# Other PSUM banks and another order for the Fourier transforms inside the Hyena layer's input projection

## What is computed

```python
def hyena_mixer(h, w_in, short_w, short_b, f_w1, f_b1, f_w2, f_b2, f_w3, f_freq, f_skip, w_out):
    seq = h.shape[1]
    v, x1, x2 = jnp.split(depthwise_conv3(h @ w_in, short_w, short_b), 3, axis=-1)
    h_freq = hyena_filters(seq, f_w1, f_b1, f_w2, f_b2, f_w3, f_freq)

    def long_conv(u, n):
        uf = u.astype(jnp.float32)
        y = jnp.fft.irfft(jnp.fft.rfft(uf, n=2 * seq, axis=1) * h_freq[:, n], n=2 * seq, axis=1)[:, :seq]
        return (y + uf * f_skip[n].astype(jnp.float32)).astype(u.dtype)

    z = x1 * long_conv(v, 0)
    z = x2 * long_conv(z, 1)
    return z @ w_out
```

## Time and profile before

| | us |
|---|---|
| median of 3 runs | 2073.58 |
| the 3 runs | 2073.58, 2074.35, 2070.02 |
| the profiled execution, its own time | 2070.28 |
| its span, first to last instruction | 2068.5 |

### The profile page before, as it was taken

One profiled execution on the slowest core, in us unless ns is written; L12 is line 12 of the kernel. 1 busy time (PEld: TensorE's weight loads), 2 busy tenths in 40 slices (PEclk: granted clock), 3 DMA queues, 4 the chain that ended last, 5 costly groups with the idle time before them and its releaser, 6 DMA issues.

```text
span 2068.5 us, 32463 instructions
## 1 busy us (share of the span) xinstructions
PE 1998.6 (97%) x12754; PEld 1619.4 (78%) x12754; DVE 1267.2 (61%) x1567; ACT 904.4 (44%) x1250; POOL 168.6 (8%) x190
## 2 busy tenths in 40 slices
PE   7989999999999999999999999999999999999999
PEld 6688678878678878978878678877767888897887
DVE  7764655557665545665667655577885554475553
ACT  4453244434544434444545544434434444444442
POOL 2242100010010001000002011002100000000000
PEclk9989999999999999999999999999999999999999
DMA  8321265545256665465455247653324555455554
GB/s 296 116 63 44 64 216 185 182 163 194 82 178 200 183 201 173 164 201 185 164 184 193 82 160 222 204 178 128 103 82 138 187 183 184 162 165 191 183 170 145
DMA packets 92752, 335.95 MB, mean 162 GB/s; under 512 B 11198, under 2 KB 11332, under 8 KB 92335
## 3 DMA queue, kind: packets, MB, share of 16 engines
q1 hardware_dynamic: 85536, 311.62, 45.3%
q0 software_dynamic: 7120, 22.95, 3.9%
HBM read 332.43 MB, written 1.05 MB: 161 GB/s over the span
## 4 chain that ended last, share of the span: by engine, by line
PE 86%; DVE 8%; POOL 2%; issue 2%; ACT 2%; DMA 0%; SPq 0%; DVEq 0%; ACTq 0%; POOLq 0%
PE acc L360 41%; PE acc L437 21%; PE acc L413 9%; PE acc L896 2%; DVE w_lo L1521 2%; PE aux L817 1%; PE aux L610 1%; PE aux L852 1%; POOL rstd L2325 1%; POOL stat L2328 1%; PE aux L884 1%; PE aux L457 1%; DVE token_scratch L1597 1%; PE aux L873 1%; DVE stat L1579 0%
## 5 line engine op out<-in xcount | busy, mean ns | idle before, releaser
L1521 DVE TENSOR_TENSOR w_lo<-w_raw,w_hi 128x1024 fp32r<-128x1024 f32 x588 | 716.3, 1224 | 583.7 <-ACT w_hi L1143 579.1
L1143 ACT ACTIVATE w_hi<-w_raw 128x1024 fp32r<-128x1024 f32 x588 | 620.2, 1059 | 798.6 <-PE acc L360 471.3
L360 PE MATMUL acc<-w_hi,operand_hi 128*128 128x512 f32 x1344 | 535.5, 398 | 26.6 <-DVE operand_lo L1676 12.2
L360 PE MATMUL acc<-w_hi,operand_lo 128*128 128x512 f32 x1344 | 526.1, 391 | 0.0
L360 PE MATMUL acc<-w_lo,operand_hi 128*128 128x512 f32 x1344 | 525.2, 391 | 0.0
L360 PEld LDWEIGHTS acc<-w_hi,operand_hi 128*128 128x128 f32 x1344 | 253.7, 189 | 88.4 <-DVE operand_lo L1542 15.0
L360 PEld LDWEIGHTS acc<-w_hi,operand_lo 128*128 128x128 f32 x1344 | 253.4, 189 | 54.4
L360 PEld LDWEIGHTS acc<-w_lo,operand_hi 128*128 128x128 f32 x1344 | 254.1, 189 | 50.6 <-issue 0.5
L437 PE MATMUL acc<-w_hi,hidden_hi 128*128 128x512 f32 x528 | 210.2, 398 | 0.0
L437 PE MATMUL acc<-w_hi,hidden_lo 128*128 128x512 f32 x528 | 208.5, 395 | 0.0
L437 PE MATMUL acc<-w_lo,hidden_hi 128*128 128x512 f32 x528 | 208.5, 395 | 0.0
(11 more groups left out here) (471 smaller groups left out, 2098.2 us busy)
## 6 DMA issues: line engine op xcount, KB each, us to landing
w_raw<-in_weights SPq DMA_DIRECT2D x588, 512.0 KB, 3.3
ln_gain<-in_gains POOLq DMA_DIRECT2D x7, 512.0 KB, 5.1
bias_at<-in_rpb POOLq DMA_DIRECT2D x12, 256.0 KB, 5.4
ln_gain<-in_ln_g POOLq DMA_DIRECT2D x4, 512.0 KB, 3.9
ln_bias<-in_ln_b POOLq DMA_DIRECT2D x4, 512.0 KB, 5.3
vec_rw<-in_vec POOLq DMA_DIRECT2D x3, 512.0 KB, 6.6
l_rw<-in_lora SPq DMA_DIRECT2D x1, 1152.0 KB, 10.6
iclr_rw<-in_xT SPq DMA_DIRECT2D x2, 512.0 KB, 4.6
```

The costliest lines, as they stand in the source:

```text
L360: mm = pe.matmul(acc[:, 2 * pair + t, :], (ah, al)[x][:, kt, t * P:(t + 1) * P], W[w][:, s, kk * 512:(kk + 1) * 512], start=(kt == 0 and ( ...
L1143: act.activation(whi[:, s, :], raw[:, s, :], ACT.Copy).then_inc(w_hi[s], 1)
L1521: dve.tensor_tensor(wlo[:, s, :], raw[:, s, :], whi[:, s, :].bitcast(F32), ALU.subtract).then_inc(w_lo[s], 1)
```

## The change

Nothing is computed that was not computed before, and no instruction is dropped. Three things differ.

1. **Banks.** Before, `turn_cv(j)` wrote HI for j = 0 to 3, LO for 4 and FAR for 5. Now it writes the banks of its own block, NEAR for an even j and FAR for an odd one. The transforms, spectra and `norm` keep to the four banks of LO and HI, but for `idft(1, 0)`, which stays in NEAR.
2. **Waits.** Since block j + 2 accumulates in the banks in which `turn_cv(j)` wrote, TensorE now waits ahead of blocks 2 and 3 for `folded`, and ahead of blocks 4 and 5 for `cv_copied` (`banks_taken`). The waits of `turn_cv(1)`, `(2)`, `(3)` and `(4)` for banks of the transforms are gone; others are moved as the banks ask for it.
3. **Order.** `norm(1)` moves from (4, 2) to (4, 1); `idft(0, 1)` with `gated(0, 1)` from (5, 0) into block 4, (4, 2); `dft(1, 0)` and `dft(1, 1)` with their products one quarter ahead, to (5, 0) and (5, 1); `spectrum(1, 1, 1)` and its butterfly from (4, 3) to (5, 2); `dft(1, 2)` behind the end of block 5.

The diff; in ScalarE's and VectorE's tables only the lines that name the places are left:

```diff
     def dft_banks(n, r):
-        return ((HI, LO, HI, LO), (HI, HI, LO, HI))[n][r]
+        return ((HI, HI, LO, HI), (HI, LO, HI, LO))[n][r]
     def idft_banks(n, c):
-        return ((LO, LO), (NEAR, LO))[n][c]
+        return ((LO, LO), (NEAR, HI))[n][c]
     def cv_banks(j):
-        return (HI, HI, HI, HI, LO, FAR)[j]
+        return (NEAR, FAR)[j % 2]
+    def spectrum_order(f, part, c):
+        return 4 + 2 * c + (1 - part) if f else 2 * (1 - part) + c
     def spectrum_banks(f, part, c):
-        return (LO, LO, LO, LO, HI, LO, HI, NEAR)[spectrum_order(f, part, c)]
-    def spectrum_order(f, part, c):
-        return 4 * f + 2 * (1 - part) + c
+        return (LO, LO, LO, LO, HI, HI, HI, LO)[spectrum_order(f, part, c)]
+    def even_of(f, part, c):
+        return EVENS[spectrum_order(f, part, c) % 2]
     def norm_bank(f):
-        return (aux[:, 0, :], acc[:, 2, :])[f]
+        return (LO, HI)[f][:, 0, :]
...
                 elif (j, i) == (2, 0):
-                    free(m["folded"])
                     dft(0, 0)
...
                 elif (j, i) == (2, 2):
-                    free(m["dft_done"])
                     turn_cv(1)
                 elif (j, i) == (2, 3):
-                    free(m["freq_done"])
+                    free(m["dft_done"])
                     dft(0, 1)
                 elif (j, i) == (3, 0):
-                    free(m["folded"])
+                    free(m["freq_done"])
                     dft(0, 2)
...
                 elif (j, i) == (3, 2):
-                    free(m["dft_done"])
                     turn_cv(2)
                 elif (j, i) == (3, 3):
                     free(m["dft_done"])
                     idft(0, 0)
                 elif (j, i) == (4, 0):
                     free(m["tap0_zeroed"])
-                    pe.wait_ge(m["cv_copied"], due(m["cv_copied"], 3))
+                    free(m["dft_done"])
                     spectrum(1, 1, 0)
+                elif (j, i) == (4, 1):
+                    free(m["freq_done"])
+                    norm(1)
                 elif (j, i) == (4, 2):
-                    free(m["freq_done"])
                     turn_cv(3)
-                    norm(1)
+                    free(m["idft_done"])
+                    idft(0, 1)
                 elif (j, i) == (4, 3):
-                    free(m["idft_done"])
-                    spectrum(1, 1, 1)
-                    free(m["cv_copied"])
+                    free(m["norm_taken"])
                     spectrum(1, 0, 0)
-                    free(m["norm_taken"])
                 elif (j, i) == (5, 0):
                     free(m["freq_done"])
-                    idft(0, 1)
+                    dft(1, 0)
                 elif (j, i) == (5, 1):
-                    free(m["freq_done"])
-                    dft(1, 0)
+                    free(m["idft_done"])
+                    dft(1, 1)
                 elif (j, i) == (5, 2):
-                    free(m["idft_done"])
                     turn_cv(4)
                     free(m["dft_done"])
-                    dft(1, 1)
+                    spectrum(1, 1, 1)
                 elif (j, i) == (5, 3):
+                    free(m["dft_done"])
                     spectrum(1, 0, 1)
-                    free(m["cv_copied"])
-                    dft(1, 2)
+            def banks_taken(j):
+                if j in (2, 3):
+                    free(m["folded"])
+                elif j >= 4:
+                    pe.wait_ge(m["cv_copied"], due(m["cv_copied"], 3 if j == 4 else 1))
...
             for j in range(6):
+                banks_taken(j)
                 block_channels(q + 4 * j, j % 2, operand_waits=(j == 0), after={i: lambda i=i: inside_block(j, i) for i in range(4)})
-            free(m["dft_done"])
+            free(m["freq_done"])
+            dft(1, 2)
+            free(m["freq_done"])
             dft(1, 3)
-            free(m["freq_done"])
+            free(m["cv_copied"])
             idft(1, 0)
...
+            def turned_and_sides():
+                copy_cv(3)
+                copy_first_half(0, 1)
+            def turned_and_spectrum():
+                copy_cv(4)
+                copy_even(1, 1, 1)
...
+                elif (j, i) == (4, 1):
+                    scale_taps(1)
                 elif (j, i) == (4, 2):
-                    scale_taps(1)
+                    gated(0, 1)
                 elif (j, i) == (4, 3):
-                    butterfly(1, 1, 1)
                     butterfly(1, 0, 0)
                 elif (j, i) == (5, 0):
-                    gated(0, 1)
+                    products(1, 0)
                 elif (j, i) == (5, 1):
-                    products(1, 0)
+                    products(1, 1)
                 elif (j, i) == (5, 2):
-                    products(1, 1)
+                    butterfly(1, 1, 1)
```

More of the change, by code:

```diff
@@ L1459, in copy_even @@
                 due(m["freq_ready"])
-                act.activation(EVENS[c], spectrum_banks(f, part, c)[:, 0, :], ACT.Copy).then_inc(m["even_copied"], 1)
+                act.activation(even_of(f, part, c), spectrum_banks(f, part, c)[:, 0, :], ACT.Copy).then_inc(m["even_copied"], 1)
             def absolute(f):
@@ L1475, in copy_first_half @@
                 act.activation(FIRST_HALF[n][c], idft_banks(n, c)[:, 0, :], ACT.Copy).then_inc(m["half_copied"], 1)
-            def two_spectra():
+            def turned_and_sides():
[3 more added lines that the diff above has]
+                copy_cv(4)
                 copy_even(1, 1, 1)
-                copy_even(1, 0, 0)
             def sides_and_spectrum():
@@ L1490, in hyena @@
             act.wait_ge(m["filt_done"], due(m["filt_done"], 0) + 4)
-            inside = {(0, 0): lambda: absolute(0), (2, 1): spectrum_and_sizes, (4, 0): sides_and_spectrum, (4, 3): two_spectra, (5, 0): lambda: copy_first_half(0, 1)}
-            inside.update({(j, 2): lambda j=j: copy_cv(j - 1) for j in range(1, 6)})
-            spectra = {(0, 1): (0, 1, 0), (0, 3): (0, 1, 1), (1, 3): (0, 0, 0), (5, 3): (1, 0, 1)}
+            inside = {(0, 0): lambda: absolute(0), (2, 1): spectrum_and_sizes, (4, 0): sides_and_spectrum, (4, 2): turned_and_sides, (5, 2): turned_and_spectrum}
+            inside.update({(j, 2): lambda j=j: copy_cv(j - 1) for j in range(1, 4)})
+            spectra = {(0, 1): (0, 1, 0), (0, 3): (0, 1, 1), (1, 3): (0, 0, 0), (4, 3): (1, 0, 0), (5, 3): (1, 0, 1)}
             inside.update({at: lambda which=which: copy_even(*which) for at, which in spectra.items()})
@@ L2174, in butterfly @@
                 odd = spectrum_banks(f, part, c)[:, 1, :]
-                kept, signed = (odd, EVENS[c]) if part else (EVENS[c], odd)
+                kept, signed = (odd, even_of(f, part, c)) if part else (even_of(f, part, c), odd)
                 for x, sign in enumerate((SGN[:], NSGN)):
```

## The result

The changed kernel takes 2075.19 us, the median of 20 runs (2070.33 to 2081.44); the kernel before took 2071.1 us beside it (20 runs, 2065.57 to 2074.35). The ratio is 1.0025, with a 95% interval of 1.0018 to 1.0033: slower by 4 to 5 us, at the very edge of what the prediction called telling. Its profiled execution took 2075.09 us with a span of 2073.3; forecast were 2073.0 us for that execution and 2076.3 for the median.

The account below looks back on a forecast made before the run. TensorE, busy for 97% of the span, was taken as the bound. Waits of 1.19 + 2.14 + 2.96 - 3.61 = +2.68 us and an even clock put the median at 2076.3 us, range 2071 to 2080.

Parts of the forecast that it names:

- What bounds, and what is removed: TensorE bounds; three waits, at `turn_cv(2)`, `turn_cv(3)` and `dft(1, 1)`, go for 3.61 us, with 1.78 us of clock.
- What is added: New TensorE waits: 1.19 us ahead of block 2, 2.14 ahead of block 3, 2.96 at `norm(1)`.
- The end of the stage taken at nothing: From `butterfly(1, 0, 1)` to `gated(1, 1)` VectorE's order is unchanged, so no time is added.
- The clock: `norm(1)`'s gap brings one stretch at 1.2 GHz, worth the 1.78 us that goes; the 1.19 and 2.14 gaps bring none.
- The sum: Whole kernel: waits of +2.68 us and an even clock make +2.7 us, a median of 2076.3 us.
- the likeliest case: Three new waits and one stretch at 1.2 GHz behind `norm(1)`: +2.7 us, chance 0.40.
- two stretches: Slower rival: the 2.14 us gap ahead of block 3 also brings a stretch at 1.2 GHz; +4.5 us, chance 0.15.
- No stretch behind `norm(1)`: Rival: no stretch at 1.2 GHz follows `norm(1)`'s gap, 1.78 us less; +0.9 us, chance 0.22.
- A longer wait at `norm(1)`: Slower rival: each us that VectorE's queue is later there costs one us more; chance 0.09.
- The folds alone: Rival: VectorE 3 us sooner at the butterfly, only the waits for the folds cost; -2.1 us, chance 0.08.
- all covered: Faster rival: the new waits are covered and 5.4 us are gone; 2068.2 us, chance 0.06.

Follow-up runs that it names:

- e4: Kernel before with its banks and order, but blocks 2 and 3 as wholes wait for the fold; ratio 1.0022 to the kernel before.
- e2: Changed kernel with `fold(0)` and `fold(1)` earlier in VectorE's order, `norm(1)` still at (4, 1); ratio 1.0018 to the kernel before.
- e1: Changed kernel with `norm(1)` and `scale_taps(1)` put back at (4, 2); ratio 1.0008 to the kernel before.
- e8: Changed kernel with three identity matmuls, their result unused, in the gap ahead of `norm(1)`; ratio 1.0020 to the kernel before.
- e9: Kernel before with three identity matmuls, their result unused, ahead of `turn_cv(2)`; ratio 1.0005 to the kernel before.
- e3: Changed kernel with both folds earlier in VectorE's order and `norm(1)` with `scale_taps(1)` at (4, 3); ratio 0.9996 to the kernel before.
- e11: The kernel of e3 once more, unaltered; ratio 0.9995 to the kernel before, median 2067.72 us.
- e6: Kernel before with six identity matmuls, their result unused, ahead of `turn_cv(2)`; ratio 0.9995 to the kernel before.
- e10: The changed kernel again, unaltered; ratio 1.0035 to the kernel before, median 2077.98 us over five runs.

## Why the prediction was right, and where a term was off

**What bounds, and what is removed:** right. `turn_cv(2)` and `dft(1, 1)` wait for nothing. What e4 adds is that the new banks had little to do with it: with the old ones, the two waits for the folds and 1.5 us of lower clock cover the old 2.9 us, the waits alone all but an estimated 0.3.

**What is added:** right to a few hundredths. The waits measure 1.21, 2.15 and 3.0 us, where 1.19, 2.14 and 2.96 were worked out, at the three places named. e2 and e1 confirm the two reasons for the third: VectorE's queue (the wait grows when TensorE comes sooner) and the place of `norm(1)` (a quarter later the wait isn't there). A small term was not counted: what follows a gap starts slowly. The quarters behind the two new gaps took 3.14 and 3.13 us instead of 2.87, but before, `turn_cv(3)` and `dft(1, 1)` took 1.10 and 1.98 instead of 0.87 and 1.72: nothing in sum.

**The end of the stage taken at nothing:** right. From the end of block 5 to the output projection it is 22.72 us (1539.97 to 1562.69), where 23 were said.

**The clock:** the mechanism was right, the size not. I let `norm(1)`'s gap bring "one such stretch, worth the same 1.78 as that which goes". It brought one, and the 2.15 us gap brought none, as said; that it brought none is luck in part, for in e4 it brought one. But the one behind `norm(1)` lasted 6.8 us and cost 3.3 and 3.2 in the two profiles of the changed kernel, and e8, which takes it away, gives 3.0 back in its profile. So the term that I put at 0 is +3.3 - 1.78 = +1.5 us. With waits of +2.75 and a tail of -0.2 this makes 4.1 us; the stage grew by 3.9. Why this stretch is twice as long as before's is not settled: both gaps are 2.9 to 3.0 us long. The removed 1.78 came in full, since TensorE is later here against VectorE: from the start of `turn_cv(2)` to the end of `idft(0, 0)` it is 7.17 us (1487.21 to 1494.38) where it was 8.97. In the kernel before alone it would have been worth 0.54, as e9 shows.

**The sum.** +2.7 us was forecast, 3.9 came in the profiled stage, 4.1 in medians and 5.2 by the ratio, whose interval (3.7 to 6.8 us) doesn't hold the forecast. The time of 2076.3 was near the measured one partly because it was counted from a median of three runs that lay 2.5 us above that of twenty. So that hit is luck in part. By stage and medians the result stands between the likeliest case and the slower rival with two stretches (+4.5), by the ratio beyond it: not by a second gap, but by one stretch of double length.

**The rivals.** *No stretch behind `norm(1)`*: falls, 6.8 us of it. *Two stretches*: falls for the changed kernel, but e4 shows that a 2.15 us gap can bring one. *A longer wait at `norm(1)`*: falls at 3.0, and e2 shows how it would come about. *The folds alone* and *all covered*: fall, the waits are there. The rule of the Trainium skill's "PSUM — Partial Sum Buffer", section "Summary: rules for kernel authors", asks for semaphores that guard by bank; every kernel here keeps it, so no run tests it, and what keeping it takes in the changed kernel is 1.21 and 2.15 us. e2 shows that these were not what the kernel lost by: without them the stage is less than 0.5 us shorter.

**What stays open.** The profiled stages of e1, e3 and e11 are 1.7, 3.1 and 1.5 us shorter than before's, and their runs show no gain that can be told; e4's is 1.3 longer, and its runs show 3 to 5. Each kernel has one profile (the changed one two, e3's two), so one stage with a stretch more or less stands against the median of many runs: the tail alone scatters by 2.2 us, and the first quarter of e11 adds 1.5 that e3 hasn't. Whether that is all of it, these runs don't say.

## What to carry to other kernels

When a shared set of buffers is split by owner, ask who is still reading them when the next owner comes, and then follow the delay along the engine with the queue: in e2 removing the new waits moved most of them to the next meeting. Price a gap on TensorE with what runs behind it until the full clock is back, as a range: behind 2.9 to 3.0 us it was 1.8 to 3.3 us here, up to as much as the gap itself. And ask what a slower clock was hiding before you count it as won.

## What the runs showed of the hardware

- Gaps of one length are followed by different clocks: 2.15 us by none in the changed kernel and by 3.4 us at 1.2 GHz in e4; 2.9 to 3.0 us by 3.4 us of it in before and 6.8 in the changed kernel. The Trainium skill, "TensorE: Matmul & The Clock Gate", section "What's actually happening", says that the moment at which the clock changes varies from run to run of one kernel. The rows of e3 and e11, one kernel, agree: behind the same idle 1.18 us their first quarter has a granted clock of 1.00 and of 0.63.
- `norm(1)`, sixteen matmuls of 64 columns, took 3.68 us behind its gap, at a granted clock of 0.50, where `norm(0)` took 1.73; and three 128x512 matmuls of the identity (each shown as two) took 2.74 us, six 5.15.
- Runs of one kernel lie up to 11 us apart, and part of that comes from ahead of the stage: it starts anywhere from 1412.55 us (e11) to 1422.41 (e6). Between e10 (1420.82) and e11 two early stretches make most of it. TensorE alone, e10 first, then e11:

```profile
100.00:150.00 50.00, 42.27 (x853) 0.84 0.21 65
...
528.00:545.00 17.00, 14.46 (x70) 0.70 0.09 32
```

```profile
100.00:150.00 50.00, 42.61 (x1123) 0.97 0.22 65
...
528.00:545.00 17.00, 16.16 (x112) 1.00 0.14 46
```

The instructions there are the same in both kernels, and the granted clock is 0.84 and 0.70 in one, 0.97 and 1.00 in the other. For a change of 4 us the stage's own length, and many runs, say more than one execution's time.
